# Opening of a hybrid decoder layer: order of the first loads, small vectors on ScalarE's queue, and token rows turned by a diagonal of 1/rms

## The reference

```
h = x * rsqrt(mean(x * x) + 1e-6) * norm_mix_g      # per token
p = h @ w_in                                        # 1024 x 2560
A (RWKV-7 time mixing), B (sliding-window attention) from p
x = x + concat(o_A, rmsnorm(o_B)) @ w_out
x = x + moe(rmsnorm(x))                             # 16 experts, each 3 matrices
y = rmsnorm(x)
```

## Time and profile before

| | us |
|---|---|
| median of 3 executions | 1232.49 |
| profiled execution | 1230.54 |
| its span | 1228.6 |
| TensorE busy | 1134.4 (92% of the span) |
| VectorE busy | 471.8 (38%) |
| ScalarE busy | 364.6 (30%) |
| GpSimd busy | 268.6 (22%) |

### The profile page before, as it was taken

The page is one execution under the profiler, slowest core; times in us unless marked ns, Lnnn a source line. Parts: engine busy times, 40 slices in busy tenths (PEclk is TensorE's granted clock), DMA queues, the critical chain, the costliest instruction groups (busy, mean ns, idle before and its releaser), DMA issues.

```text
span 1228.6 us, 25098 instructions
## 1 busy us (share of the span) xinstructions
PE 1134.4 (92%) x10940; PEld 804.8 (66%) x10940; DVE 471.8 (38%) x963; ACT 364.6 (30%) x816; POOL 268.6 (22%) x163
## 2 busy tenths in 40 slices
PE   6999999999999787877799999789999999999995
PEld 4666666656566666756554544488778887887883
DVE  3200656366764667565634322631011110101143
ACT  3101545445433456453521311111101111111152
POOL 0000000001110299999300000111212111112103
PEclk9999999999999999998999999889999999999998
DMA  6511100010110300002331741177889988999963
GB/s 199 152 35 37 54 18 18 18 35 23 37 39 1 67 4 5 4 13 45 91 106 49 280 175 69 56 270 258 285 295 313 306 279 304 347 319 339 375 263 114
DMA packets 96410, 175.00 MB, mean 142 GB/s; under 512 B 20394, under 2 KB 41709, under 8 KB 95892
## 3 DMA queue, kind: packets, MB, share of 16 engines
q1 hardware_dynamic: 88708, 152.11, 35.9%
q0 software_dynamic: 7584, 21.20, 6.6%
HBM read 148.30 MB, written 28.41 MB: 144 GB/s over the span
## 4 chain that ended last, share of the span: by engine, by line
PE 86%; DVE 9%; issue 3%; ACT 2%; SPq 0%; DMA 0%; POOLq 0%; POOL 0%; DVEq 0%
PE ps L754 22%; PE ps L1454 21%; PE ps L1254 9%; PE ps L1479 9%; PE ps L1485 2%; PE ps L833 1%; PE ps L857 1%; PE ps L846 1%; PE ps L1430 1%; PE ps L970 1%; PE ps L1011 1%; DVE ps L2310 1%; PE ps L958 1%; PE ps L1317 1%; DVE arena L2299 1%
## 5 line engine op out<-in xcount | busy, mean ns | idle before, releaser
L754 PE MATMUL ps<-arena 128*128 128x355 f32 x960 | 299.6, 468 | 1.9 <-issue 1.7
L1454 PEld LDWEIGHTS ps<-arena 128*128 128x128 f32 x2048 | 257.6, 192 | 11.6 <-issue 11.6
L1454 PE MATMUL ps<-arena 128*128 128x160 f32 (+4 forms) x2048 | 260.3, 289 | 4.9 <-issue 4.9
L754 PEld LDWEIGHTS ps<-arena 128*128 128x128 f32 x960 | 180.2, 191 | 107.4 <-issue 10.3
L1254 PE MATMUL ps<-arena 128*128 128x512 f32 x256 | 116.6, 597 | 0.9 <-DVE arena L2373 0.7
L1479 PE MATMUL ps<-arena 128*128 128x512 f32 x256 | 113.5, 595 | 0.8 <-DVE arena L2648 0.8
L2648 DVE TENSOR_TENSOR arena<-arena,ps 128x160 f32<-128x160 f32 (+4 forms) x64 | 19.5, 305 | 227.2 <-ACT arena L1983 227.2
L1983 ACT ACTIVATE arena<-ps 128x160 f32<-128x160 f32 (+4 forms) x64 | 18.7, 292 | 295.3 <-PE ps L1454 295.3
L2832 POOL TENSOR_TENSOR arena<-arena 128x1024 f32<-128x1024 f32 x4 | 11.4, 2856 | 329.6 <-DVE arena L2174 329.6
L1479 PEld LDWEIGHTS ps<-arena 128*128 128x128 f32 x256 | 47.2, 190 | 54.3 <-issue 53.0
L1574 ACT COPY arena<-ps 128x355 f32<-128x355 f32 x60 | 27.2, 453 | 183.7 <-PE ps L754 183.7
(11 more groups left out here) (414 smaller groups left out, 1585.3 us busy)
## 6 DMA issues: line engine op xcount, KB each, us to landing
arena<-in_w_exp_gate SPq DMA_DIRECT2D x16, 2048.0 KB, 11.0
arena<-in_w_exp_up SPq DMA_DIRECT2D x16, 2048.0 KB, 17.4
arena<-in_w_exp_down SPq DMA_DIRECT2D x16, 2048.0 KB, 15.6
arena<-in_w_in SPq DMA_DIRECT2D x16, 512.0 KB, 3.9
arena<-in_x_prompt SPq DMA_DIRECT2D x9, 512.0 KB, 3.8
x_dram<-arena SPq DMA_DIRECT2D x9, 512.0 KB, 3.6
h_dram<-arena SPq DMA_DIRECT2D x8, 512.0 KB, 2.6
out_y_prompt<-arena SPq DMA_DIRECT2D x8, 512.0 KB, 3.8
```

The source lines that it names most:

```text
L754: last = pe.matmul(ps[:, q % 2, 0:m], wr[:, n % 3, k, :], hT[:, k, a:a + m], start=(k == 0), stop=(k == KB - 1))
L1454: last = pe.matmul(ps[:, 3 + f % 2, n * CAP:n * CAP + CAPS[e]], w[a][:, k, f * P:(f + 1) * P], xgT[:, a, k, 0:CAPS[e]], start=(k == 0), st ...
```

## The change

Five edits, all in the opening:
- SyncE asks for tile 0 first, then for the table of constants, then for tile 1; the table has the semaphore const_ok, on which TensorE and VectorE now wait, and which also takes over what vec_ok did.
- The eleven small vectors are asked for by ScalarE, at the head of its program.
- ScalarE then takes a root of one constant column into an unused column of stat, ahead of the first norm. norm(1) comes ahead of the copy of the vectors.
- VectorE writes no scaled rows: it writes diag, the identity times 1/rms (two buffers of 128x128), and TensorE multiplies the unscaled rows with it. For tiles 2 and later VectorE first waits until the tile two before is turned.
- VectorE clears a 512-column block, and TensorE multiplies it with itself four times ahead of the turn of the vectors, into a PSUM bank that nothing reads.

```diff
-            sp.dma_start(table[:, :], i["c_table"]).then_inc(s["vecs_in"], 16)
...
-            for t in range(2):
-                load_x(t)
-            at = 0
-            for n, k in zip(VECS, VEC_ROWS):
...
-                sp.dma_start(dst, src).then_inc(s["vecs_in"], 16)
-                at += k
-
+            load_x(0)
+            sp.dma_start(table[:, :], i["c_table"]).then_inc(s["const_ok"], 16)
+            load_x(1)
...
-            pe.wait_ge(s["vecs_in"], 16 + 16 * len(VECS))
-            nv = sum(VEC_ROWS)
-            pe.transpose(ps[:, 7, 0:nv], vecs_rows[:, :], ident[0:nv, 0:nv]).then_inc(s["vec_ps"], 1)
+            def warm(n):
+                for _ in range(n):
+                    pe.matmul(ps[:, 6, 0:512], blank[:, 0:P], blank, start=True, stop=True)
+
+            def vecs_turn():
+                pe.wait_ge(s["vecs_in"], 16 * len(VECS))
+                nv = sum(VEC_ROWS)
+                pe.transpose(ps[:, 7, 0:nv], vecs_rows[:, :], ident[0:nv, 0:nv]).then_inc(s["vec_ps"], 1)
+
+            pe.wait_ge(s["dve"], 1)
+            warm(4)
+            pe.wait_ge(s["const_ok"], 16)
+            vecs_turn()
...
-                        last = pe.transpose(ps[:, 2 + 2 * (t % 2) + j, k * n:(k + 1) * n], xt[0:n, t % 4, (4 * j + k) * P:(4 * j + k + 1) * P],
-                                            ident[0:n, 0:n])
+                        last = pe.matmul(ps[:, 2 + 2 * (t % 2) + j, k * n:(k + 1) * n], xt[0:n, t % 4, (4 * j + k) * P:(4 * j + k + 1) * P],
+                                         diag[0:n, t % 2, 0:n], start=True, stop=True)
...
         def _(act):
+            at = 0
+            for n, k in zip(VECS, VEC_ROWS):
...
+                act.dma_start(dst, src).then_inc(s["vecs_in"], 16)
+                at += k
+            act.wait_ge(s["dve"], 1)
+            act.activation(stat[:, 60:61], eps[:, 0:1], ACT.Sqrt)
+
...
             norm(0)
+            norm(1)
             act.wait_ge(s["vec_ps"], 1)
-            act.copy(vecs[:, :], ps[:, 7, 0:sum(VEC_ROWS)]).then_inc(s["vec_ok"], 1)
-            for t in range(1, 5):
+            act.copy(vecs[:, :], ps[:, 7, 0:sum(VEC_ROWS)]).then_inc(s["const_ok"], 1)
+            for t in range(2, 5):
                 norm(t)
...
-                dve.tensor_scalar(xt[0:n, t % 4, :], xt[0:n, t % 4, :], stat[0:n, 30 + t:31 + t], None, ALU.mult).then_inc(s["h_ok"], 1)
+                if t >= 2:
+                    dve.wait_ge(s["hT_ps"], 2 * (t - 1))
+                dve.tensor_scalar(diag[0:n, t % 2, 0:n], ident[0:n, 0:n], stat[0:n, 30 + t:31 + t], None, ALU.mult).then_inc(s["h_ok"], 1)
...
             dve.memset(eps[:, 1:2], LNX_EPS)
+            link(dve.memset(blank, 0.0))
+            dve.wait_ge(s["const_ok"], 16)
             x_scale(0)
```

More of the change, by code:

```diff
@@ L46 @@
 FIRST = 0
-CHAIN0, CHAIN1 = 139, 180
+CHAIN0, CHAIN1 = 140, 181
 LAST = 3
@@ L68 @@
 ARENA = 20 * W + KB * W + HP * W1 + 15504
-SEMS = """vecs_in shift_in x0 x1 x2 x3 sumsq ms_ok std_ok h_ok hT_ps hT_ok vec_ps vec_ok w0 w1 w2 p_ps p_ok
+SEMS = """vecs_in shift_in x0 x1 x2 x3 sumsq ms_ok std_ok h_ok hT_ps hT_ok vec_ps const_ok w0 w1 w2 p_ps p_ok
 prev_ok dve mixed lora_act lora_ps gates_ok kk_sq kk_ps kk_ms kk_std bonus_in bonus_ps exps scaled
@@ L196, in program @@
         levelf = part(KN0 + P, 2 * LV * CH)
+        diag = part(KN0 + P + 2 * LV * CH, 2 * P).rearrange("p (s c) -> p s c", s=2)
+        blank = part(KN0 + 3 * P + 2 * LV * CH, 512)
         shin = part(SH0, SHIFT_W)[0:DB, :]
@@ L1558, in _ @@
         def _(act):
+            at = 0
+            for n, k in zip(VECS, VEC_ROWS):
+                dst = vecs_rows[at:at + k, :]
+                src = i[n]
+                if n == "r_k":
+                    src = src[0].rearrange("(a b) d -> a (b d)", b=2)
+                elif n == "attn_norm_g":
+                    src = src[0].rearrange("(kv g d) -> g kv d", kv=2, g=GRP)
+                    dst = dst.rearrange("g (kv d) -> g kv d", kv=2)
+                else:
+                    src = src[0].rearrange("(a b) -> a b", b=P)
+                act.dma_start(dst, src).then_inc(s["vecs_in"], 16)
+                at += k
+            act.wait_ge(s["dve"], 1)
+            act.activation(stat[:, 60:61], eps[:, 0:1], ACT.Sqrt)
             def norm(t):
@@ L1713, in _ @@
                     act.wait_ge(s["vec_ps"], 2)
-                    act.copy(shT[:, :], ps[:, 7, P:P + 14 * DB]).then_inc(s["vec_ok"], 1)
-                    act.wait_ge(s["vec_ok"], 2)
+                    act.copy(shT[:, :], ps[:, 7, P:P + 14 * DB]).then_inc(s["const_ok"], 1)
+                    act.wait_ge(s["const_ok"], 18)
                 elif h == 37:
@@ L2115, in x_turned @@
                 if t == 0:
-                    dve.wait_ge(s["vec_ok"], 1)
+                    dve.wait_ge(s["const_ok"], 17)
                 for j in range(2):
```

## The result

| | median | runs | ratio to before, 95% interval |
|---|---|---|---|
| before | 1230.21 us (1221.91 to 1239.23) | 16 | |
| after | 1235.77 us (1232.56 to 1241.89) | 16 | 1.0052 (1.0033 to 1.0072) |
| after, a second time | 1243.58 us, beside 1237.29 of before | 12 | 1.0051 (1.0025 to 1.0077) |

By this ratio the change makes the kernel slower by 6.4 us (4.1 to 8.9); the two medians lie 5.6 us apart. Forecast were 1.6 us less. The median of after lies in the forecast range, within 1% of before, but the sign of the shift is wrong. The profiled execution of after took 1236.45 us for a span of 1234.3 (before: 1230.54 and 1228.6).

A forecast was written before the change was run, and what follows sets the result against it. TensorE's stream was taken as the bound (86% of the span). Terms -3.35 - 2.67 - 0.38 + 4.82 = -1.6 us gave 1231.0 from the 1232.49 median; range 1227 to 1236, within 1% at 0.96.

The forecast's parts named there:

- Start of the projection: Opening: first projection starts at 15.05 us instead of 18.40, 3.35 earlier, through ScalarE's prologue, the diagonal and norm 1 ahead.
- the vectors' landing: Opening: the small vectors, last asked for on ScalarE's queue at 4.3 us, land at about 7.6, by today's 3.35.
- Forecast slack: Vectors may land up to 0.6 us later, since tile 0's turn may start at 8.7 without VectorE waiting.
- so there is room: Opening: DMA engines had emptied at 6 to 8 us (176 GB/s against 408 before), leaving room for earlier requests.
- Rival 2: ScalarE's requests cost more than 0.35 us each; at GpSimd's 1.0 the kernel is 5.5 slower, 1238; chance 0.14.
- Clock: First projection half runs at 2.4 GHz after the clear matmuls: 2.40 us in place of 5.07, 2.67 less.
- Turns: Tiles 3 to 8: fp32 matmul turns take 16 records, 1.79 us against 0.87, together 4.82 us more.
- rival 3: The turns cost no more than now, about 4 of the 4.82 us are won: 1227; chance 0.12.
- Waits: TensorE's waits on VectorE between 18.40 and 43.60 us vanish: 0.38 us less.
- that all behind 43.60 only moves along: After the last turn's end at 43.60 us, moving TensorE's stream moves the kernel's end; no term for later stages.
- Rival 4: Later stages: a moved start may meet the clock's falls otherwise, 1.5 us either way, with any other; no separate chance.
- Rival 1: Opening: clear matmuls don't raise the clock: +0.4, 1232.9, or 1238 if turns don't either; chance 0.14 (0.03 the 1238).

## Why the prediction was wrong

**Start of the projection: -3.35 forecast, -1.66 came.** The steps on ScalarE held: a request takes 0.32 to 0.37 (the first 0.60) for the 0.35 taken, the first square starts at 6.42 (6.1), the second at 8.00, the diagonal takes 0.29 (0.23), VectorE's cycle is 2.02 (1.95), and no load stands behind the square. The first failed step is the vectors' landing: I took SyncE's 3.35 us and had them at 7.6; they landed at 9.53, 4.87 after the last request, and in four more traces with the vectors on this queue after 5.32 to 5.56. Forecast slack was 0.6, for a turn of tile 0 at 8.7 at the latest; it began at 9.9. The step under it was "so there is room": I read the gap in the DMA at 6 to 8 us, and did not ask who would fill it. The same sentence had the tiles and weights asked for 2 to 4 us sooner, and they did fill it (396 GB/s for 176). Whether the other queue or this traffic makes the small transfers late was not parted. Rival 2 named the right queue, but the price per request, on which it rested, was not what cost.

**Clock: -2.67 forecast, -2.44 came** in the profiled pair. As a mean over executions it is less: before's first eight projection records took 5.07, 5.07, 5.07, 4.31, 4.30, 3.86 and 2.63 in seven traces, 4.33 on average, so about -1.7 (-2.1 without the last two, which had 64 and 40 tiny matmuls ahead). One profile's clock is one draw. And it is the diagonal turns, not the clear matmuls, that keep the clock up to the projection: all five traces with them have 2.63 there, with or without the clear matmuls, and only two of the fifteen with transposes; the clear matmuls save the turns' own slow start.

**Turns: +4.82 forecast, +5.45 came.** A turn of 16 records took 1.78, as taken; rival 3 is refuted. The mis-sized part is tile 8, which took 1.90 and not 1.22: its records have 32 columns, and the weight loads are busy nearly throughout (1.86 us), but why a record takes 0.12 here and 0.08 as a transpose is open. **Waits: -0.38**, as forecast.

By the opening alone the forecast should have been +0.9 for this pair: 1.7 of the 2.5 us missed are the late start, 0.6 the turns, 0.2 the clock. For the mean over executions it should have been +2.9. That the median still lies in the forecast range is luck: its upper part was there for slow requests and for a clock that stays down, and neither came.

**The second failed step: that all behind 43.60 only moves along.** Of the 8.0 us between forecast and measured, the opening has 4.5 by the mean of the traces (2.5 in the profiled pair), and this step the other 3.5. I counted 80 more matmul records as time on TensorE and not as program. In the chain of waits the pieces named "issue" of 0.4 us and more between 407 and 640 us sum to 7.2 to 9.7 us in the five traces with before's number of records (mean 8.3), and to 9.9 to 15.6 in the fifteen with more (mean 12.2), with no overlap; with the shorter pieces it is 17.5 to 20.0 and 20.3 to 25.4. One place stands out: between 410 and 445 us none of the five has such a wait of 1 us or more, and ten of the fifteen have one. The chain of after, pieces of this kind above 2 us:

```profile
428.21 3.42 issue
...
562.67 3.46 issue
...
621.66 2.73 issue
```

and of before run again, all above 1 us:

```profile
453.39 1.37 issue
...
505.18 1.37 issue
...
559.70 2.19 issue
...
614.68 2.40 issue
```

In whole times of the kernels with tiny matmuls alone it is less, 2.0 us (single ratios 1.0009 to 1.0030, only one of the four told from nothing by itself). So of the 6.4 us, 2.9 are the opening, 2 to 3 the added records, and up to 1.5 stay open, inside the interval. That the waits are for the program is inferred from the times of the packets; why 16 more records already do it was not found, nor whether more of them do more. Rival 4 (the clock's later falls) is there in every trace at other places and of other length. Part of it goes with the waits: the clock of after falls at 431.28, at the end of the wait of 3.4 us. Between 407 and 640 us the clock stands at 1.2 GHz for 6.8 to 20.5 us in the five traces (mean 15.0) and for 17.1 to 34.1 in the fifteen (mean 22.3); the ranges overlap, and what of the loss is the wait and what the clock behind it was not told apart.

**Rival 1** was partly right: clear matmuls raise the clock (8 records from 1.52 to 6.74, done before the forecast 7.6), but with a pause or transposes behind them it falls back. In after TensorE stood idle for 2.9 us behind them and the clock held; in the second run of after it was 3.7, and the clock fell at 11.4; in the kernel after with transposes it was 2.9 again, and the clock fell at 9.7 all the same. That transposes mostly don't hold it agrees with the Trainium skill ("TensorE: Matmul & The Clock Gate", Part 4), which says that transpose mode does not count as TensorE being busy in the same way. Against its strict reading: in the kernel after with transposes the clock rose at 16.5 us, when only transposes had run since it fell at 9.7, and in the trace of the 40 tiny matmuls at 16.0 us, when only transposes and tiny matmuls had run.

## What to carry to other kernels

- Price an fp32 turn by a true matmul at twice the records of a transpose before trading VectorE's time for it: where TensorE is the bound, 0.91 us more per tile on its path outweighs the 0.5 us saved on an engine that has time.
- Moving small requests off a busy queue brought the requests forward here, not the landing; take the landing from a row with the same bulk traffic beside it, ask what the change itself puts into a gap before counting on it, and give the slack a bound of its own. The cheap gain here was order: first rows first, vectors turned behind tile 0, and the one VectorE step that the projection wants ahead of one that waits for rows.
- Instructions added to TensorE ahead of a stretch of many short matmuls had a cost in this kernel, 2 to 3 us in the mean, and 16 records were enough for some of it. And a claim of 1 us from one profile needs to know how far that term differs between executions; here the clock alone moved it by 2.4.

## What the runs showed of the hardware

- Eleven small transfers on ScalarE's queue beside bulk on SyncE's landed 4.87 to 5.56 us after the last request, in five traces; on SyncE's queue itself 2.96 to 3.52, in ten traces in which less bulk was asked for by then.
- The table load of 1.28 us on an idle ScalarE had nothing behind it: the next instruction started 0.02 us later (after, 5.02 to 6.32).
- A 128x128 fp32 turn by a diagonal: 1.78 us for 16 records; with 32 columns 1.90, where the transposes take 0.87 and 0.61.
- From 407 to 640 us TensorE's path has 7 to 16 us of waits of 0.4 us and more for nothing that the profile names. The 98 of 1 us and more, in twenty traces, each end 1.2 to 1.8 us after a packet of the instruction queue; the 35 of 2 us and more all have data packets beside it. Such a wait of 3.4 us was followed by a granted clock of 0.62.
